# Two-block transformer on one core: band bias made earlier, a long convolution summed in PSUM, SSD low halves on VectorE

## The reference

```python
proj = u @ w_in
y_a = conformer_conv_branch(glu, w (31 taps), ...) @ w_conv_out   # depthwise causal convolution, 31 taps
y_b = ssd_branch(z, xbc, dt, ...) @ w_ssd_out                     # state space, 16 channel tiles, gated by silu(z)
y_c = swa_branch(q, k, v, ..., rel_bias, band_dist) @ w_attn_out  # 16 heads, band of 128 keys, relative bias
gates = sigmoid(proj[gates] + gate_bias)
h = h + (gates[0] * y_a + gates[1] * y_b + gates[2] * y_c) @ w_mix_out
```

## Time and profile before

| | us |
|---|---|
| median of 3 runs (lowest to highest) | 3452.19 (3443.16 to 3452.74) |
| the profiled execution | 3452.04 |
| its span | 3449.9 |
| PE busy | 3131.0 (91%) |
| DVE busy | 1262.4 (37%) |
| ACT busy | 1270.0 (37%) |
| POOL busy | 1632.0 (47%) |

### The profile page before, as it was taken

One profiled execution on the slowest core, in us unless ns is written; L12 is line 12 of the kernel. 1 busy time (PEld: TensorE's weight loads), 2 busy tenths in 40 slices (PEclk: granted clock), 3 DMA queues, 4 the chain that ended last, 5 costly groups with the idle time before them and its releaser, 6 DMA issues.

```text
span 3449.9 us, 48315 instructions
## 1 busy us (share of the span) xinstructions
PE 3131.0 (91%) x19966; PEld 2731.7 (79%) x19966; DVE 1262.4 (37%) x2283; ACT 1270.0 (37%) x2176; POOL 1632.0 (47%) x826
## 2 busy tenths in 40 slices
PE   7999999988888999999999989789958978689899
PEld 5777878778888777787788877688955976589899
DVE  2222035434444322202222055241498775131380
ACT  3222243244444322223222245343434344145453
POOL 3333443344342533344344441588851761377587
PEclk9999999999999999999999999899977985689999
DMA  5444224300000244423433220654431440134254
GB/s 208 165 167 157 92 98 147 125 27 1 1 1 1 82 163 171 153 92 116 171 104 104 91 86 19 136 200 154 165 116 44 153 147 1 43 119 162 99 181 161
DMA packets 96890, 381.54 MB, mean 111 GB/s; under 512 B 10368, under 2 KB 15648, under 8 KB 87200
## 3 DMA queue, kind: packets, MB, share of 16 engines
q1 hardware_dynamic: 87456, 311.33, 26.5%
q10 hardware_dynamic: 9216, 67.11, 5.5%
HBM read 374.21 MB, written 4.19 MB: 110 GB/s over the span
## 4 chain that ended last, share of the span: by engine, by line
PE 77%; DVE 11%; ACT 4%; DMA 3%; POOL 3%; issue 2%; SPq 0%; ACTq 0%; DVEq 0%; POOLq 0%
PE bank L219 20%; PE bank L220 19%; PE bank L221 19%; DVE cv L1439 6%; PE bank L713 6%; PE bank L292 2%; POOL weights_lo L212 1%; DVE norm_work L409 1%; DMA weights_landing<-w_up 1%; PE bank L1307 1%; PE bank L719 1%; PE bank L365 1%; DMA skew<-by_dist 1%; DVE norm_work L403 1%; PE bank L303 1%
## 5 line engine op out<-in xcount | busy, mean ns | idle before, releaser
L212 POOL TENSOR_TENSOR weights_lo<-weights_landing,weights_hi 128x1024 fp32r<-128x1024 f32 x554 | 1331.3, 2407 | 1383.6 <-ACT weights_hi L202 1383.4
L202 ACT ACTIVATE weights_hi<-weights_landing 128x1024 fp32r<-128x1024 f32 x554 | 586.4, 1059 | 1529.9 <-PE bank L221 1422.8
L219 PE MATMUL bank<-normed_hi,weights_lo 128*128 128x256 f32 (+1 forms) x2864 | 987.9, 345 | 84.0 <-ACT weights_hi L202 29.9
L220 PE MATMUL bank<-normed_lo,weights_hi 128*128 128x256 f32 (+1 forms) x2864 | 966.2, 337 | 0.0
L221 PE MATMUL bank<-normed_hi,weights_hi 128*128 128x256 f32 (+1 forms) x2864 | 964.8, 337 | 0.0
L219 PEld LDWEIGHTS bank<-normed_hi,weights_lo 128*128 128x128 f32 x2864 | 554.7, 194 | 170.9 <-POOL normed_lo L425 31.2
L221 PEld LDWEIGHTS bank<-normed_hi,weights_hi 128*128 128x128 f32 x2864 | 554.2, 193 | 57.5
L220 PEld LDWEIGHTS bank<-normed_lo,weights_hi 128*128 128x128 f32 x2864 | 555.4, 194 | 49.2
L219 PE MATMUL bank<-hidden_hi,weights_lo 128*128 128x512 f32 (+1 forms) x960 | 331.7, 345 | 4.1 <-POOL weights_lo L212 4.1
L221 PE MATMUL bank<-hidden_hi,weights_hi 128*128 128x512 f32 (+1 forms) x960 | 328.9, 343 | 0.0
L220 PE MATMUL bank<-hidden_lo,weights_hi 128*128 128x512 f32 (+1 forms) x960 | 328.7, 342 | 0.0
(11 more groups left out here) (394 smaller groups left out, 4091.6 us busy)
## 6 DMA issues: line engine op xcount, KB each, us to landing
weights_landing<-w_up SPq DMA_DIRECT2D x176, 512.0 KB, 3.3
ada_landing<-w_ada ACTq DMA_DIRECT2D x64, 1024.0 KB, 4.8
weights_landing<-w_down SPq DMA_DIRECT2D x88, 512.0 KB, 3.2
weights_landing<-w_dn SPq DMA_DIRECT2D x33, 512.0 KB, 3.2
weights_landing<-w_mlp_up SPq DMA_DIRECT2D x32, 512.0 KB, 3.2
weights_landing<-w_mlp_down SPq DMA_DIRECT2D x32, 512.0 KB, 3.2
weights_landing<-w_gate SPq DMA_DIRECT2D x24, 512.0 KB, 3.3
weights_landing<-w_xbc SPq DMA_DIRECT2D x24, 512.0 KB, 3.2
```

Source lines behind the costliest of these rows:

```text
L202: k.nc.scalar.activation(k.WH[:, u % SLOTS, :], k.W[:, u % LANDS, :], ACT.Copy).then_inc(*k.AC.mark(("unit hi", u)))
L212: k.nc.gpsimd.tensor_tensor(k.WL[:, u % SLOTS, :], k.W[:, u % LANDS, :], k.WH[:, u % SLOTS, :].bitcast(F32), ALU.subtract).then_inc(*k.PO. ...
L219: nc.tensor.matmul(out, ll, rh, start=start, stop=False, skip_group_check=True)
L220: nc.tensor.matmul(out, lh, rl, start=False, stop=False, skip_group_check=True)
```

## The change

Four things are edited; 31 x 8 taps, all products and all values stay.

1. The band bias is made in the first attention. `band_pe` stands at query tile 5 of `window_project_pe`, in bank 7 instead of 6, `band_act` at query tile 6. `rel` moves in front of w_swa_q. The two DMAs are split: the write in front of unit 4 of w_swa_out, the shifted read in front of unit 6. The mask on GpSimd stands behind the low halves of w_swa_q and in front of those of w_swa_out. swa_cols moves in SBUF, since biasm now lives beside it.
2. The long convolution sums in banks 6 and 7 in turn, and a copy to cv ends each channel tile.
3. It is issued in two places: five tiles behind glu, three behind attn out, and no more in the rounds of the attention. TensorE waits for the fifth tile in front of v, because v uses bank 6.
4. The low halves of y in ssd out are made on VectorE, one tile behind the scaling.

```diff
@@ places
-        self.rt1, self.cols1 = f("swa_turned", 88, 2, TOK), f("swa_cols", 92, 2, 8, 4)
+        self.rt1, self.cols1 = f("swa_turned", 88, 2, TOK), f("swa_cols", 115, 2, 8, 4)
@@ window_project_pe
     linear(k, pe, st + " k", w.streams[0], 2, KT, lambda d: [t[:, d, 0:w.n_tokens] for t in x], w.n_tokens,
            before, ready, first=2)
+    if not w.rope:
+        pe.wait_ge(*k.DV.after("conv", 4))
     for d in range(KT):
         wv = tile_parts(k, pe, w.streams[1], d, 256)
...
             q_turn(n - 3)
+        if w.rope and n == 5:
+            pe.wait_ge(*k.DV.after(st, "k roped", 1))
+            band_pe(k, pe)
@@ window_project_act
+        if w.rope and n == 6:
+            band_act(k, act)
@@ long_conv
-        x, y = k.gl[:, at, :], k.cv[:, at, :]
+        x, y, z = k.gl[:, at, :], k.B[6 + at % 2][:, 0:LAT], k.cv[:, at, :]
...
+        dve.wait_ge(*k.DV.after("conv", at, 0))
+        nc.vector.tensor_copy(z, y).then_inc(*k.DV.mark(("conv", at)))
+        yield
@@ band_pe, band_act: k.B[6] becomes k.B[7]; band_sp becomes two functions
-def band_sp(k, sp):
-    skew = k.nc.dram_tensor(f"skew{int(k.counted)}", [P, 16, 384], F32, kind="Internal").ap()
+def band_rows_sp(k, sp, skew):
     sp.wait_ge(*k.AC.after("band", "by_dist"))
     sp.dma_start(skew.rearrange("i h x -> h i x"),
                  k.by_dist[0:16, :].unsqueeze(1).to_broadcast([16, P, 384])).then_inc(k.skewed, 16)
+
+
+def band_shift_sp(k, sp, skew):
     sp.wait_ge(k.skewed, 16)
...
@@ ssd_out_pe: linear waits for k.DV.after("ssd", "y lo", d) instead of k.PO.after(...)
@@ ssd_out_dve
+    def low(t):
+        dve.wait_ge(*k.AC.after("ssd", "y hi", t))
+        nc.vector.tensor_tensor(k.y_lo[:, t, :], k.xbc[:, t, :], k.y_hi[:, t, :].bitcast(F32), ALU.subtract).then_inc(*k.DV.mark(("ssd", "y lo", t)))
+
     for t in range(INNER):
...
+        if t:
+            low(t - 1)
+    low(INNER - 1)
@@ ssd_out_pool
-    for t in range(INNER):
-        pool.wait_ge(*k.AC.after("ssd", "y hi", t))
-        k.nc.gpsimd.tensor_tensor(k.y_lo[:, t, :], k.xbc[:, t, :], k.y_hi[:, t, :].bitcast(F32), ALU.subtract).then_inc(*k.PO.mark(("ssd", "y lo", t)))
-        if t % 2:
-            feed_pool(k, pool, k.F.ahead("w_ssd_out", 4 * (t + 1)))
     feed_pool(k, pool, k.F.ahead("w_ssd_out", KT * INNER))
@@ pe_program, act_program
-    mlp_pe(k, pe, "mlp11", lambda n: band_pe(k, pe) if n == 4 else None)
+    mlp_pe(k, pe, "mlp11")
-    mlp_act(k, act, "mlp11", lambda n: band_act(k, act) if n == 5 else None)
+    mlp_act(k, act, "mlp11")
@@ dve_program
     conv = long_conv(k, dve)
-    take(conv, 110)
-    window_project_dve(k, dve, attn, lambda n: take(conv, 3))
+    take(conv, 5 * (CONV + 1))
+    window_project_dve(k, dve, attn)
     dve.wait_ge(*k.PO.after("band", "masked", 3))
-    window_heads_dve(k, dve, attn, band_mask(k), lambda n: take(conv, 5))
+    window_heads_dve(k, dve, attn, band_mask(k))
     for n in range(KT):
         branch_out_dve(k, dve, "attn out", 16, n)
-    take(conv, KT * CONV)
+    take(conv, 3 * (CONV + 1))
@@ pool_program
     feed_pool(k, pool, k.F.ahead("w_swa_q", KT * KT))
+    band_pool(k, pool)
     out_pool(k, pool, "w_swa_out", KT)
     norm("norm12", lat)
-    mlp_pool(k, pool, "mlp11", lambda: band_pool(k, pool))
+    mlp_pool(k, pool, "mlp11")
@@ sp_program
-    late = {F.base["w_dn"] + 27: level, F.base["w_down10"] + 10: rope, F.base["w_swa_out"]: rel,
-            F.base["w_up11"] + 16: lambda: band_sp(k, sp), F.base["w_mix"] - 1: mem}
+    skew = k.nc.dram_tensor(f"skew{int(k.counted)}", [P, 16, 384], F32, kind="Internal").ap()
+    late = {F.base["w_dn"] + 27: level, F.base["w_down10"] + 10: rope, F.base["w_swa_q"]: rel,
+            F.base["w_swa_out"] + 4: lambda: band_rows_sp(k, sp, skew),
+            F.base["w_swa_out"] + 6: lambda: band_shift_sp(k, sp, skew), F.base["w_mix"] - 1: mem}
```

More of the change, by code:

```diff
@@ L1485, in band_pe @@
     pe.wait_ge(k.rel_landed, 48)
-    k.nc.tensor.matmul(k.B[6][0:16, 0:384], k.rel[0:32, :], k.bucket[0:32, :], start=True, stop=True).then_inc(*k.PE.mark(("band", "by_dist")))
+    k.nc.tensor.matmul(k.B[7][0:16, 0:384], k.rel[0:32, :], k.bucket[0:32, :], start=True, stop=True).then_inc(*k.PE.mark(("band", "by_dist")))
 def band_act(k, act):
     act.wait_ge(*k.PE.after("band", "by_dist"))
-    k.nc.scalar.activation(k.by_dist[0:16, :], k.B[6][0:16, 0:384], ACT.Copy).then_inc(*k.AC.mark(("band", "by_dist")))
-def band_sp(k, sp):
-    skew = k.nc.dram_tensor(f"skew{int(k.counted)}", [P, 16, 384], F32, kind="Internal").ap()
+    k.nc.scalar.activation(k.by_dist[0:16, :], k.B[7][0:16, 0:384], ACT.Copy).then_inc(*k.AC.mark(("band", "by_dist")))
+def band_rows_sp(k, sp, skew):
     sp.wait_ge(*k.AC.after("band", "by_dist"))
@@ L1832, in ssd_out_pe @@
     linear(k, pe, "ssd out", "w_ssd_out", KT, INNER, lambda d: (k.y_hi[:, d, :], k.y_lo[:, d, :]), LAT,
-           lambda n: k.DV.after("ssd out", "ev", n - 4) if n >= 4 else None, lambda d: k.PO.after("ssd", "y lo", d), first=4, beside=beside)
+           lambda n: k.DV.after("ssd out", "ev", n - 4) if n >= 4 else None, lambda d: k.DV.after("ssd", "y lo", d), first=4, beside=beside)
 def ssd_out_act(k, act):
```

## The result

The changed kernel takes 3359.15 us (median of 4 runs, 3349.89 to 3359.95), the kernel before 3452.47 on the same chip (3443.16 to 3453.42). The ratio is 0.9729, with a 95% interval of 0.9713 to 0.9746: 93.3 us less. The profiled execution took 3359.7 us with a span of 3357.6; the two spans are 92.3 us apart. I had forecast 3358.

The account below looks back on a forecast made before the run. TensorE carries three quarters of the chain of waits, standing idle behind VectorE's long convolution and the skew DMA. Terms 32.8 + 27.5 + 4.5 + 8.8 + 17.6 + 2.5 = 93.7 us, from 3452.0 to 3358; 8-in-10 range 3336 to 3382.

Parts of the forecast that it names:

- Part 1: Band bias moved from mlp11 to the first attention: 31.8 + 6.0 gained, 5 lost to masks, 32.8 us net.
- the masks cost: First attention's heads: VectorE's SBUF-only work waits behind four GpSimd masks; 5 us lost, between 0 and 9.6.
- Part 2a: Five convolution tiles in banks beside the gates: query tile 1 starts earlier, 27.5 us gained; 15.7 to 31 by step time.
- the step in a bank: Long convolution on VectorE: 0.504 us a step when summing in a bank, between 0.48 and 0.58.
- The wait before v: Second attention: TensorE newly waits about 7 us for the fifth convolution tile, then runs at 1.2 GHz.
- The prediction's 10.7 us: Convolution beside the gates: by the skill's fixed cost for bank sources, five tiles would end 10.7 us later; the trace disagreed.
- Part 2b: Second attention without filling convolution steps: 4.5 us in the projection's tail (3 to 5), 8.8 in eight heads (0 to 19).
- Part 2c: Three convolution tiles beside z: TensorE's wait at xbc goes, all but half a microsecond, 17.6 us gained.
- Part 3: SSD output product, low halves of y on VectorE, still blocked behind GpSimd's conversion: 2.5 us gained, 0 to 4.
- The unit wait: SSD output product: TensorE's wait in each weight unit falls from 4.30 to 3.9 us.
- The first rival: SSD output product: y_lo slips ahead of GpSimd, gaining 18.5 us instead of 2.5, up to 15 more by clock; 10%.
- Part 2: Convolution moved into banks and two places: 27.5 us beside the gates, 4.5 and 8.8 without fills, 17.6 beside z.

Follow-up runs that it names:

- experiment 6: Changed kernel with the band mask made as a 33rd row of the bucket product, no GpSimd mask instructions: 3349.09 us, ratio 0.9699 to the kernel before.
- experiment 1: Changed kernel with the convolution summing in SBUF again, without the copy, its two places kept: 3441.52 us, ratio 0.9957 to the kernel before.
- experiment 5: Changed kernel with the convolution's banks exchanged, so v waits for its fourth tile, not the fifth: 3350.3 us, ratio 0.9701 to the kernel before.
- experiment 8: Changed kernel with five spare convolution steps as dead work in each of the second attention's 8 heads: 3372.17 us, ratio 0.9766 to the kernel before.
- experiment 4: Changed kernel with ACT making all 16 high halves of y before converting the next weights: 3317.2 us, ratio 0.96 to the kernel before.

## Why the prediction was right

**Part 1: 32.8 forecast, 32.1 measured.** The rows DMA was issued at 2052.89 (forecast 2052.5) and had landed at 2085.07 (2085); the masks ended at 2104.5 (2108), with 46 us to spare. The query loads were issued 10.06 us later than before and nobody waited: the queries start at 2035.7 in place of 2035.9. Only the sizes inside the sum were off: mlp11 gave 38.4 (forecast 31.8 + 6.0 = 37.8), and the masks cost 7.8, as experiment 6 shows (I took 5 between 0 and 9.6; the 2.1 lost at the low clock behind them I had not thought of). The table has 6.3 because the kernel after had gained 1.3 before the third head's scores, ahead of the masks, where eight of its matmuls took 1.15 us in place of 1.97. No term stood for that, so part of the agreement here is luck.

**Part 2a: 27.5 forecast, 26.5 measured** (58.6 - 32.1). The choice that mattered was the step in a bank: 0.504 taken between 0.48 and 0.58, 0.507 measured. The blocking is gone, as L535 had said, and experiment 1 shows that without the bank it is back. A tile took 16.16 us from start to start (forecast 16.0), since the tensor_scalar that writes a bank took 0.54 in place of the 0.41 of the earlier trace rows. The wait before v was 7.90 (forecast 7), and experiment 5 shows that it cost about 10 us at v. The Trainium skill, page "VectorE: DVE Perf Modes", section "The TRN2 errata — SBUF-src ops pay a fixed extra latency per instruction", gives 120 cycles of fixed cost from a bank to SBUF against 58 from SBUF to SBUF. The trace doesn't show this difference for the form used here: a step that reads one bank operand and one from SBUF, and writes the same bank, has a median of 473 ns, as the all-SBUF step has. (The prediction's 10.7 us by that rule counts 165 steps; in the five tiles 155 instructions read a bank, which makes 10, again an estimate from that page.)

**Part 2b: 4.5 and 8.8 forecast, 3.5 and 11.4 measured.** The mechanism was right, both sizes a little off, in opposite directions. In the heads I had counted only the part of the fill that outlasted ACT's sum (1.1 us a head); experiment 8 shows that such a fill costs 1.5 a head.

**Part 2c: 17.6 forecast, 18.5 measured.** No wait of TensorE at xbc is left, and it also got the half microsecond that I had kept back.

**Part 3: 2.5 forecast, 3.4 measured.** The unit wait is 3.91 (forecast 3.9), and the subtraction is blocked in each unit, as forecast. It ends 0.28 us after the conversion (forecast 0.27). The Trainium skill, page "SBUF — State Buffer", section "Who interferes with whom", says that a VectorE instruction with two SBUF inputs contends with a GpSimd one that reads SBUF, and that the order of issue decides which one is blocked. The trace agrees: 2.36 us, behind a conversion that began first, for an instruction that takes 0.41 alone. The first rival, y_lo ahead of GpSimd, didn't occur. But its price, 18.5 us and up to 15 more from the clock, pointed at a real loss that the prediction left alone: experiment 4 got 42 by another way, reordering ACT, that I hadn't looked for.

**The sum: 93.7 forecast, 95.4 at the last place that the change touches, 92.4 at the end.** What I had no term for is the stretch from ln_silu to cross_k, 70.5 us before and 76.1 after, with the same instructions. Inside it, a stretch of the kernel after and that with the same distance from ln_silu in the kernel before:

```profile
2983.60:2988.60 5.00, 5.00 (x24) 5.00 (x25) 0.00 (x0) 1.07 (x2) 2.70 (x2) 0.50 0.52 188
```

```profile
3079.00:3084.00 5.00, 5.00 (x43) 5.00 (x43) 0.92 (x3) 2.72 (x4) 3.25 (x3) 1.00 0.47 161
```

TensorE is busy all the time in both, with 24 matmuls at a granted clock of 0.50 (1.2 GHz) against 43 at 1.00. Over that part the clock is 0.88 after and 0.93 before:

```profile
2954.60:3055.00 100.40, 90.31 (x669) 89.55 (x668) 22.86 (x47) 51.57 (x89) 74.44 (x48) 0.88 0.38 134
```

```profile
3050.00:3145.00 95.00, 84.52 (x671) 83.76 (x671) 22.91 (x47) 51.84 (x89) 74.77 (x49) 0.93 0.41 142
```

The loss is 5.6 us, 2.6 of it come back later. The first is no scatter of one profile: all nine experiments have 74.6 to 76.8 us there, though the kernel before has only the one trace. The 2.6 may be scatter: from cross_k to the output the experiments take 303.1 to 306.6 us, the kernel before 305.9 and the one after 303.3. Why the clock fell at other matmuls in the two kernels was not settled; no experiment varied it alone. So that the sum came within 1.3 us is in part luck, the errors cancel: the terms missed by -0.7, -1.0, -1.0, +2.6, +0.9 and +0.9, together +1.7, and the clock by -3.0.

## What to carry to other kernels

A VectorE accumulation beside GpSimd's conversions can run at its own speed if the sum lives in a spare bank, so that only one operand comes from SBUF. With the convolution placed as it is here, the bank was worth 80 us; against the kernel before, all of Part 2 gave 60. Where the bank is wanted next decides what is left of it (some 7 to 10 us by which of two banks the last tile used). Before moving an operation to a faster engine, look at which instruction stands in front of its producer: the move gained 3.4 us, one `if` less on ACT gained 42. A short repeated wait costs more than its length, 41 us for seven waits of 3.9, because the matmuls behind each run at half the clock.

## What the hardware showed that I had not expected

- A tensor_scalar that writes a bank took 0.54 us at 256 elements (536 to 541 ns in all eight) against 0.41 into SBUF, while scalar_tensor_tensor shows no difference (473 ns both). In experiment 8 the first of them, right behind a memset, took 0.41 too; why is open.
- TensorE, busy without a gap, still ran 24 matmuls in 5 us at a granted clock of 0.50, where the same part of the kernel before had 1.00; the same instruction stream differed by 5.6 us.
- Where a tensor_scalar with a single SBUF tensor input writes decides whether GpSimd blocks it. Into SBUF it was blocked: 2565 ns against 482 beside the masks, and 1.99 us against 0.41 beside a conversion in the kernel before. Into a bank it was not: 536 to 541 ns, with four of the eight wholly inside a conversion.
- The masks cost 2.1 us more after they had ended, when TensorE's matmuls ran at the low clock behind a wait of 4.42 us.
